# Router of a hybrid decoder layer: squares summed on VectorE, all expert groups ranked at once, bfloat16 counts, first rows picked on TensorE

## The chip, the cores and the metric

The program runs on one core of one Trainium2 chip, in one launch. The metric is the device time in microseconds (us) of that core. Engines are written as in the profile: PE is TensorE (PEld its weight loads), DVE is VectorE, ACT is ScalarE, POOL is GpSimd, SP is SyncE, which here issues most of the transfers. A trailing q (ACTq, SPq) marks the issue of a transfer.

## The reference, cut to what matters

One layer of a decoder on 264 tokens (256 of a prompt, 8 to be decoded) with 1024 channels. Two recurrent mixers run side by side, their outputs go through one projection of 2048 to 1024 and are added to the residual stream. Then comes the part that the change touches, a mixture of 16 experts in 4 groups of 4:

```python
def hier_moe(h, ...):                      # h = rmsnorm(x) * w_norm_ffn
    glog = (t @ w_rg).astype(f32)          # 264 x 4
    gprob = softmax(glog); gsel = argmax(glog + b_rg)
    gw = gprob at gsel
    elog = (t @ w_re) of the chosen group  # 264 x 4
    eprob = softmax(elog)
    _, topi = lax.top_k(elog + b_re[gsel], 2)
    ew = eprob at topi, divided by its sum
    gates = one_hot(4 * gsel + topi) * gw * ew
    act = silu(t @ w_gate[e]) * (t @ w_up[e]) * gates[e]     # 512 wide
    return sum over e of act @ w_down[e]
```

So each token chooses one group, then two of its four experts. After the experts a small gated embedding is added, and a last RMSNorm gives the output. All inputs and outputs are float32.

## The kernel before, in words

Each engine has its own program, written by hand; the order in the source is the order on the engine, and semaphores join them. Channels stand on the 128 partitions in most of the kernel: `xT`, `hT` and `sq` are 8 tiles (KT) of 128 x 264, one for each 128 channels. PSUM banks are handed out in turn: banks 0 to 3 go from PE to ACT (`a_full`, `a_took`), banks 4 to 7 from PE to DVE (`v_full`, `v_took`).

**Output projection (mix).** For each c of 8 output tiles PE multiplies 16 weight tiles into a bank (L1048, which appears as 32 instructions, two for each float32 product). DVE adds the bank to `xT[c]` and scales it into `hT[c]` (`weighted`); ACT writes the square of `xT[c]` to `sq[c]`. For the RMSNorm PE sums the squares over channels by a matrix of ones: `norm_part(1, c)`, L806, once for each of the 8 tiles, all into one bank. Four of these stand between the last mix tiles and four behind them, with the router's own products (`router_part`, L1067, 20 columns: 4 groups and 16 experts). ACT takes the root (L1364), PE turns the 1/rms factors and the router's logits so that tokens stand on partitions (L1102, L1074), and turns `hT` back to rows (`h_row`, L1094). ACT scales these rows into `htok`, two copies for each of three token tiles (L1572), and sends them to `h_rows` in HBM.

**Choice of experts.** DVE works on tiny arrays: 3 token tiles by 4 or 16 numbers on 128 partitions. `link` makes each instruction wait until the one before it has written. First the group is chosen (`first_max`: the maximum, who equals it, the first of these), then the four logits of that group are gathered, then the best and the second best are found, again with `first_max`. `Mt` holds for each token and expert whether it was chosen. PE counts with it (`cnt`, L1114): how many earlier tokens chose each expert, which is a token's slot there. Meanwhile DVE works out the gates and fills `rv`, the numbers that belong to each token and expert. Then, for each expert t, DVE compares slot numbers with 1 to 64 in two copies (`one_hots`, `OH`, 8 buffers) and PE multiplies `OH` with `rv` (`table`, L1123), which gives for every slot the token's row number and gate. Table 0 holds experts 0 and 1 (TAB0 = 2), table 1 the other 14. DVE copies each (L2023) and turns it into row numbers (`row_numbers`, semaphore `tab_ready`).

**Experts.** Up to 64 slots (CAP) for each expert. POOL gathers an expert's rows by an indirect transfer from `h_rows` into `xg` (L743) as half rows, 128 partitions of 512. PE turns them (`halves_rows`, L1235, bank 2 or 3), ACT copies them to `xgT` (L1540, `x_took`), PE multiplies with gate and up weights (`halves_gate_up`, L1226, `gu_full`), ACT and DVE make silu times up times gate, PE turns that and multiplies with the down weights (L1256, `d_full`). POOL scatters the result (L751). PE enters this phase by a wait for `v_took` of table 1.

**Weights.** An expert's three matrices are 6 MB. There are three slots (SLOTS). The first three experts' weights are asked for during the mix. From the fourth on SP waits for PE:

```python
for t in range(SLOTS, E):
    eng.wait_ge(main.gu_full, t - SLOTS + 1)
    load_gate(t)
    load_up(t)
    eng.wait_ge(main.d_full, t - SLOTS + 1)
    load_down(t)
```

## Time and profile before

| | us |
|---|---|
| median of 3 runs (lowest, highest) | 736.98 (734.15, 738.41) |
| time of the profiled execution | 739.89 |
| its span, first to last instruction | 738.1 |
| PE busy | 654.5 (89%) |
| PE weight loads busy | 451.9 (61%) |
| DVE busy | 297.4 (40%) |
| ACT busy | 178.8 (24%) |
| POOL busy | 82.3 (11%) |
| mean granted TensorE clock | 0.948 |

The time of an execution holds 1.8 us outside the span. Busy shares are means over stages with very different limits: the mixers and the projection lie before about 410 us, the router from there to 438.6 us, the experts from there to about 670 us, and the closing part behind them. A granted clock of 1.00 is TensorE's full 2.4 GHz, 0.50 is 1.2 GHz.

### The profile page before, as it was taken

The page shows a single profiled execution, that of the slowest core. Times are in us where ns is not written, and L with a number is a line of the kernel's source. Part 1 is how long each engine was busy: PE and PEld are TensorE (multiplying, and loading weights), DVE is VectorE, ACT ScalarE, POOL GpSimd, SP SyncE. Part 2 cuts the span into 40 slices and gives each one's busy share as a digit, 9 for nine tenths or more (in the row PEclk, how much of TensorE's full clock was granted, in tenths as well). Part 3 has the DMA queues.
Part 4 walks back from the last instruction along what each step waited for, and adds up shares of the span by engine and source line. Part 5 has one row for each costly group of instructions (what it writes and reads, how often), then busy time and mean ns, then how long its engine had stood idle before and what let it go on. Part 6 is the DMA issues. An engine that isn't in the chain of part 4 may idle for free. (4 is left out here: it accounts for less than half of the span.)

```text
span 738.1 us, 8341 instructions
## 1 busy us (share of the span) xinstructions
PE 654.5 (89%) x3225; PEld 451.9 (61%) x3225; DVE 297.4 (40%) x863; ACT 178.8 (24%) x417; POOL 82.3 (11%) x103
## 2 busy tenths in 40 slices
PE   4899999999998999999999759998877778786896
PEld 2688887787786988888877533332322223234685
DVE  0368277864449899845210570010001000010443
ACT  3222338312232232343300511010100000011323
POOL 5000024200012111100000010211111111001000
PEclk9999899999998999899999959999999999998899
DMA  9634258983023645535897705999999999996001
GB/s 252 232 114 133 97 176 282 345 266 132 1 88 103 214 131 180 166 92 172 342 377 306 284 25 235 407 422 423 424 423 422 421 427 422 426 398 222 0 1 59
DMA packets 44978, 177.92 MB, mean 241 GB/s; under 512 B 3989, under 2 KB 12633, under 8 KB 36608
## 3 DMA queue, kind: packets, MB, share of 16 engines
q1 hardware_dynamic: 34704, 147.21, 51.0%
q0 software_dynamic: 9712, 28.99, 12.7%
q10 hardware_dynamic: 520, 1.15, 0.4%
q8 instruction: 27, 0.44, 0.3%
q14 instruction: 15, 0.12, 0.0%
HBM read 165.48 MB, written 16.01 MB: 246 GB/s over the span
## 5 line engine op out<-in xcount | busy, mean ns | idle before, releaser
L830 PE MATMUL bank<-hT,arena 128*128 128x264 f32 x832 | 197.3, 398 | 5.7 <-DVE hT L1636 3.1
L830 PEld LDWEIGHTS bank<-hT,arena 128*128 128x128 f32 x832 | 161.9, 197 | 35.2 <-issue 5.6
L1226 PE MATMUL bank<-arena,hT 128*64 128x512 f32 x512 | 124.7, 643 | 31.0 <-DMA arena<-in_w_exp_up 30.4
L1226 PEld LDWEIGHTS bank<-arena,hT 128*64 128x64 f32 x512 | 42.2, 148 | 102.4 <-issue 100.7
L1628 DVE TENSOR_TENSOR arena<-arena 128x256 f32<-128x256 f32 (+8 forms) x149 | 60.2, 447 | 44.0 <-ACT arena L1441 20.4
L1636 DVE SCALAR_TENSOR_TENSOR hT<-hT,arena,bank 128x256 f32<-128x256 f32 x16 | 7.7, 481 | 158.8 <-ACT hT L1547 158.8
L1048 PE MATMUL bank<-arena 128*128 128x264 f32 x256 | 58.3, 387 | 1.3 <-issue 0.8
L1256 PE MATMUL bank<-arena,sq 128*64 128x512 f32 x256 | 58.4, 598 | 0.5 <-ACT sq L1552 0.5
L1048 PEld LDWEIGHTS bank<-arena 128*128 128x128 f32 x256 | 48.3, 190 | 10.6 <-issue 1.7
L1384 ACT ACTIVATE arena<-bank 128x264 f32<-128x264 f32 x44 | 17.1, 390 | 141.4 <-PE bank L830 141.3
L1547 ACT ACTIVATE hT<-bank 128x256 f32<-128x256 f32 x16 | 6.1, 384 | 147.8 <-PE bank L1226 147.8
L1636 DVE SCALAR_TENSOR_TENSOR arena<-arena 128x128 f32<-128x128 f32 (+1 forms) x130 | 35.5, 343 | 7.7 <-DMA arena<-in_state_ssm 7.5
L751 POOL DMA_INDIRECT pair_rows<-arena,rows x16 | 16.1, 1009 | 188.1 <-DVE arena L2093 188.1
L1256 PEld LDWEIGHTS bank<-arena,sq 128*64 128x64 f32 x256 | 17.3, 136 | 30.8 <-issue 30.1
L1628 DVE TENSOR_TENSOR arena<-bank,K 128x512 f32<-128x512 f32 (+1 forms) x34 | 22.4, 678 | 25.6 <-PE bank L975 15.3
L2093 DVE COPY arena<-bank 128x512 f32<-128x512 f32 x16 | 11.1, 692 | 52.3 <-PE bank L1256 52.3
L1314 PE MATMUL bank<-hT,arena 128*128 128x264 f32 x128 | 31.3, 405 | 0.0
L1855 DVE TENSOR_REDUCE arena<-arena 128x128 f32<-128x1024 f32 x16 | 30.5, 1904 | 0.0
L975 PE MATMUL bank<-arena 128*128 128x128 f32 x224 | 27.7, 275 | 1.5 <-DVE arena L1628 1.5
L1314 PEld LDWEIGHTS bank<-hT,arena 128*128 128x128 f32 x128 | 25.6, 201 | 4.7
L975 PEld LDWEIGHTS bank<-arena 128*128 128x128 f32 x224 | 26.8, 192 | 2.3 <-DVE arena L1628 1.9
L1636 DVE SCALAR_TENSOR_TENSOR arena<-arena,prm 128x253 f32<-128x253 f32 (+3 forms) x80 | 25.7, 365 | 2.4 <-ACT arena L1494 1.2
(252 smaller groups left out, 683.5 us busy)
## 6 DMA issues: line engine op xcount, KB each, us to landing
arena<-in_w_exp_gate SPq DMA_DIRECT2D x16, 2048.0 KB, 26.8
arena<-in_w_exp_up SPq DMA_DIRECT2D x16, 2048.0 KB, 31.2
arena<-in_w_exp_down SPq DMA_DIRECT2D x16, 2048.0 KB, 24.3
arena<-in_w_in SPq DMA_DIRECT2D x13, 2048.0 KB, 9.1
out<-arena POOLq DMA_DIRECT2D x18, 512.0 KB, 4.8
arena<-in_w_out SPq DMA_DIRECT2D x4, 2048.0 KB, 9.5
arena<-in_state_ssm POOLq DMA_DIRECT2D x8, 512.0 KB, 8.0
arena<-in_state_hgrn POOLq DMA_DIRECT2D x8, 512.0 KB, 4.5
```

The source lines that it names most:

```text
L751: eng.indirect_dma_start(out=pair_halves, out_offset=bass.IndirectOffsetOnAxis(ap=row_of[:, 1, t:t + 1], axis=0), in_=ys[:, p], in_offset= ...
L830: last = mm(ps[:, 0:T], w[:, k, j * P:(j + 1) * P], hT[:, k], start=(k == 0), stop=(k == KT - 1))
L975: last = mm(ps[:, j * P:(j + 1) * P], x, y, start=True, stop=True)
L1048: last = mm(ps[:, 0:T], w[:, k, (c % 2) * P:(c % 2) * P + P], x, start=(k == 0), stop=(k == 15))
L1226: last = mm(bank[p][r, :].rearrange("p (w f) -> p w f", w=2), xgT[:, p, k % 4, CAP * (k // 4):CAP * (k // 4) + CAP], gu[:, :, k, FF // 2 * ...
L1256: last = mm(bank[6 + p][r, :], actT[:, p, k % 2, CAP * (k // 2):CAP * (k // 2) + CAP], wd[:, k, HALF * c:HALF * (c + 1)], start=(k == 0), ...
L1314: last = mm(ps[:, 0:T], w[:, k, (c % 4) * P:(c % 4 + 1) * P], hT[:, k], start=(k == 0), stop=(k == KT - 1))
L1384: activation(PR[:, n], full("proj", n)[:, 0:T], func).then_inc(a_took, 1)
L1628: return nc.vector.tensor_tensor(out, a, b, op)
L1636: return nc.vector.scalar_tensor_tensor(out, a, s, b, op0, op1)
L1855: nc.vector.tensor_reduce(AT[:, h % 2, 256 * i:256 * i + P], LVt[:, i].rearrange("p a c -> p c a"), AX.X, ALU.add).then_inc(at_ready, 1)
L2093: nc.vector.tensor_copy(ys[:, p], bank[6 + p][:, :]).then_inc(main.d_took, 1)
```

## The change: what it does

1. `norm_part(1, c)` is gone. DVE adds `sq[1]` to `sq[7]` into `sq[0]` one by one (`add_square`, after ACT's square and with a semaphore `sq_sum` between them), and PE multiplies once with the ones.
2. `counting` is a bfloat16 copy of the two 128 x 128 matrices used for counting, made by DVE ahead of the mix. `Mt` is bfloat16 and has a fourth, empty tile. The count is four products with 64, 48, 32 and 16 columns in place of nine float32 products of 16.
3. DVE ranks the experts inside all four groups at once, on 48 numbers for each partition, while it ranks the groups; `pair` issues two independent instructions and waits for both. What belongs to the chosen group is masked out afterwards (`first`, `second`). The exponent's input of the expert softmax (`rs[:, 8]`, second `r_in`) comes behind the eleventh pair.
4. The slot numbers `slot1` are computed right behind the count, ahead of the gates.
5. The first expert's rows are neither gathered nor turned. DVE writes a one-hot matrix `first_hot` (3 token tiles x 64 slots, into `xg`), and PE multiplies the rows `htok` with it, 8 channel tiles x 3 token tiles = 24 float32 products of 64 columns, straight into bank 2. Half of them stand ahead of table 0, half behind it. They wait for ACT's last copy of `htok` and for `first_ready`. POOL no longer gathers for t = 0.

```diff
--- before.py
+++ after.py
@@ -344,11 +344,13 @@
         rv = carve(3 * E * RV // 2).bitcast(BF16).rearrange("p (t e c) -> p t e c", t=3, c=RV)
-        Mt = carve(3, E)
+        Mt = carve(4 * E // 2).bitcast(BF16).rearrange("p (t e) -> p t e", e=E)
...
         tabf = smalls[:, 0:3 * E * RV].rearrange("p (t c) -> p t c", c=RV)
+        counting = smalls[:, 3 * E * RV:3 * E * RV + P].bitcast(BF16)
+        first_hot = xg[:, 0, 0:3 * CAP].rearrange("p (t s) -> p t s", t=3)
@@ -356,6 +358,8 @@
         actT = sq_all[:, 1536:2048].rearrange("p (s k c) -> p s k c", s=2, k=2)
+        pick = [sq_all[:, 1536 + 3 * E * i:1536 + 3 * E * (i + 1)].rearrange("p (t g e) -> p t g e", t=3, g=EG)
+                for i in range(4)]
@@ -438,6 +442,7 @@
         sq_done, norm_done = sem("sq_done"), sem("norm_done")
+        sq_sum, counting_ready, first_ready = sem("sq_sum"), sem("counting_ready"), sem("first_ready")
@@ -758,7 +763,7 @@
                         eng.wait_ge(tab_ready, 2)
-                    if t < E:
+                    if 0 < t < E:
@@ -1077,14 +1082,14 @@
                 mix(c, range(16))
-                norm_part(1, c - 4)
...
                         router_part(k)
-            for c in range(4, KT):
-                if c >= 6:
-                    router_part(c)
-                norm_part(1, c)
+            for c in range(6, KT):
+                router_part(c)
+            ps = open_a("norm", 1)
+            eng.wait_ge(sq_sum, KT - 1)
+            mm(ps[:, 0:T], ones, sq[:, 0], start=True, stop=True).then_inc(a_full, 1)
@@ -1106,13 +1111,14 @@
-            eng.wait_ge(mt_ready, 3)
+            eng.wait_ge(counting_ready, 1)
+            eng.wait_ge(mt_ready, 2)
             ps = open_v("cnt")
-            for i in range(4):
-                c = slice(E * i, E * i + E)
-                for k in range(min(i + 1, 3)):
-                    last = mm(ps[:, c], ones if k < i else K[:, K_CAUSAL:K_CAUSAL + P], Mt[:, k],
-                              start=(k == 0), stop=(k == min(i, 2)))
+            up_to, every = counting[:, 0:P], counting[:, P:2 * P]
+            mm(ps[:, 0:4 * E], up_to, Mt[:, :, :], start=True, stop=False, skip_group_check=True)
+            for i in range(3):
+                last = mm(ps[:, E * (i + 1):4 * E].rearrange("p (t e) -> p t e", e=E), every,
+                          Mt[:, i:i + 1].to_broadcast([P, 3 - i, E]), start=False, stop=(i == 2), skip_group_check=True)
@@ -1123,7 +1129,16 @@
-            table(open_v("tab", 0), 0, TAB0, oh_ready, oh_used, v_full)
+            eng.wait_ge(a_took, ja["ht", 2, 1] + 1)
+            eng.wait_ge(first_ready, 1)
+            for k in range(KT):
+                if k == KT // 2:
+                    table(open_v("tab", 0), 0, TAB0, oh_ready, oh_used, v_full)
+                at = P * (k % 4) + CAP * (k // 4)
+                for i, (t0, n) in enumerate(TOK):
+                    last = mm(bank[2][:, at:at + CAP], htok[0:n, i, k * P:(k + 1) * P], first_hot[0:n, i],
+                              start=(i == 0), stop=(i == 2))
+            last.then_inc(main.x_full, 1)
@@ -1230,7 +1245,7 @@
                 p = t % 2
-                eng.wait_ge(main.rows[p], t // 2 * 16 + 16)
+                eng.wait_ge(main.rows[p], (t + p) // 2 * 16)
@@ -1259,7 +1274,6 @@
-                halves_rows(0)
@@ -1272,7 +1286,6 @@
-            eng.wait_ge(a_took, ja["ht", 2, 1] + 1)
@@ -1901,11 +1914,23 @@
                 tt(o[:, h], o[:, h], ms[:, h]).then_inc(mixed, 1)
+            eng.wait_ge(mixers_done, 1)
+            nc.vector.tensor_copy(counting, K[:, K_CAUSAL:K_CAUSAL + 2 * P]).then_inc(counting_ready, 1)
+            def add_square(c):
+                eng.wait_ge(sq_done, KT + c + 1)
+                if c > 1:
+                    eng.wait_ge(sq_sum, c - 1)
+                tt(sq[:, 0], sq[:, 0], sq[:, c], ALU.add).then_inc(sq_sum, 1)
...
                     weighted(c - 1, "mix", R_FFN)
+                if c >= 2:
+                    add_square(c - 1)
             weighted(KT - 1, "mix", R_FFN)
+            add_square(KT - 1)
@@ -1914,19 +1939,22 @@
-            def first_max(out, x, tmp, m):
-                red(m, x, ALU.max)
-                link(tt(tmp, x, bc(m), ALU.is_equal))
-                link(tt(tmp, tmp, w4))
-                red(m, tmp, ALU.max)
-                link(tt(out, tmp, bc(m), ALU.is_equal))
+            def pair(a, b, chain=dve):
+                for x in (a, b):
+                    own[chain] += 1
+                    x.then_inc(chain, 1)
+                eng.wait_ge(chain, own[chain])
+            def top(out, x, op):
+                return nc.vector.tensor_reduce(out, x, AX.X, op)
+            def of_group(x):
+                return x.rearrange("p t (g o) -> p t g o", o=1).to_broadcast([P, 3, EG, EPG])
...
             link(nc.vector.memset(rt[:, :, :], 0.0))
-            eng.wait_ge(mixers_done, 1)
-            for i in range(3):
-                link(nc.vector.memset(Mt[:, i], 0.0))
+            link(nc.vector.memset(Mt[:, :, :], 0.0))
@@ -1934,31 +1962,45 @@
             took("rt")
-            lg = rt[:, :, 0:4]
-            red(r1[:, 0], lg, ALU.max)
+            w16 = K[:, K_W4:K_W4 + 4].rearrange("p (o g e) -> p o g e", o=1, g=1).to_broadcast([P, 3, EG, EPG])
+            lg, ex = rt[:, :, 0:4], rt[:, :, 4:20].rearrange("p t (g e) -> p t g e", g=EG)
+            rbg = rb[:, 0:4].rearrange("p (o e) -> p o e", o=1).to_broadcast([P, 3, 4])
+            rbe = rb[:, 4:20].rearrange("p (o g e) -> p o g e", o=1, g=EG).to_broadcast([P, 3, EG, EPG])
+            biased, eq, first, second = pick
+            best, turn = rs[:, 11], rs[:, 12]
+            ohg = rs[:, 5]
+            ohb = ohg.rearrange("p t (g o) -> p t g o", o=1).to_broadcast([P, 3, EG, EPG])
+            g4 = gates[:, :, :].rearrange("p t (g e) -> p t g e", g=EG)
+            pair(top(r1[:, 0], lg, ALU.max), tt(biased, ex, rbe, ALU.add))
             tt(rs[:, 0], lg, bc(r1[:, 0]), ALU.subtract).then_inc(r_in, 1)
-            link(tt(rs[:, 3], lg, rb[:, 0:4].rearrange("p (o e) -> p o e", o=1).to_broadcast([P, 3, 4]), ALU.add))
-            ohg = rs[:, 5]
-            first_max(ohg, rs[:, 3], rs[:, 4], r1[:, 3])
-            g4 = gates[:, :, :].rearrange("p t (g e) -> p t g e", g=EG)
-            ohb = ohg.rearrange("p t (g o) -> p t g o", o=1).to_broadcast([P, 3, EG, EPG])
-            link(tt(g4, rt[:, :, 4:20].rearrange("p t (g e) -> p t g e", g=EG), ohb))
-            red(rs[:, 7], g4.rearrange("p t g e -> p t e g"), ALU.add)
-            link(tt(g4, rb[:, 4:20].rearrange("p (o g e) -> p o g e", o=1, g=EG).to_broadcast([P, 3, EG, EPG]), ohb))
-            red(rs[:, 14], g4.rearrange("p t g e -> p t e g"), ALU.add)
-            red(r1[:, 6], rs[:, 7], ALU.max)
+            pair(top(best, biased, ALU.max), tt(rs[:, 3], lg, rbg, ALU.add))
+            pair(tt(eq, biased, of_group(best), ALU.is_equal), top(r1[:, 3], rs[:, 3], ALU.max))
+            pair(tt(eq, eq, w16), tt(rs[:, 4], rs[:, 3], bc(r1[:, 3]), ALU.is_equal))
+            pair(top(turn, eq, ALU.max), tt(rs[:, 4], rs[:, 4], w4))
+            pair(tt(first, eq, of_group(turn), ALU.is_equal), top(r1[:, 4], rs[:, 4], ALU.max))
+            pair(stt(biased, first, -BIG, biased, ALU.mult, ALU.add), tt(ohg, rs[:, 4], bc(r1[:, 4]), ALU.is_equal))
+            pair(top(best, biased, ALU.max), tt(g4, ex, ohb))
+            pair(tt(eq, biased, of_group(best), ALU.is_equal), top(rs[:, 7], g4.rearrange("p t g e -> p t e g"), ALU.add))
+            pair(tt(eq, eq, w16), top(r1[:, 6], rs[:, 7], ALU.max))
+            pair(top(turn, eq, ALU.max), tt(first, first, ohb))
             tt(rs[:, 8], rs[:, 7], bc(r1[:, 6]), ALU.subtract).then_inc(r_in, 1)
-            link(tt(rs[:, 11], rs[:, 7], rs[:, 14], ALU.add))
-            first_max(rs[:, 12], rs[:, 11], rs[:, 4], r1[:, 3])
-            link(stt(rs[:, 13], rs[:, 12], -BIG, rs[:, 11], ALU.mult, ALU.add))
-            first_max(rs[:, 15], rs[:, 13], rs[:, 4], r1[:, 3])
-            link(tt(rs[:, 16], rs[:, 12], rs[:, 15], ALU.add))
-            chosen = rs[:, 16].rearrange("p t (o e) -> p t o e", o=1).to_broadcast([P, 3, EG, EPG])
-            for i, (t0, n) in enumerate(TOK):
-                tt(Mt[0:n, i].rearrange("p (g e) -> p g e", g=EG), ohb[0:n, i], chosen[0:n, i]).then_inc(mt_ready, 1)
+            link(tt(second, eq, of_group(turn), ALU.is_equal))
+            link(tt(second, second, ohb))
+            tt(Mt[:, 0:2].rearrange("p t (g e) -> p t g e", g=EG), first[:, 0:2], second[:, 0:2], ALU.add).then_inc(mt_ready, 1)
+            tt(Mt[0:NS, 2].rearrange("p (g e) -> p g e", g=EG), first[0:NS, 2], second[0:NS, 2], ALU.add).then_inc(mt_ready, 1)
+            ps = full("cnt")
+            eng.wait_ge(mt_ready, 2)
+            link(tt(slot1[:, :, :], ps[:, 0:3 * E].rearrange("p (t e) -> p t e", e=E), Mt[:, 0:3]))
+            eng.wait_ge(xg_clear, 2)
+            tt(first_hot, K[:, K_IOTA:K_IOTA + CAP].rearrange("p (o s) -> p o s", o=1).to_broadcast([P, 3, CAP]),
+               slot1[:, :, 0:1].to_broadcast([P, 3, CAP]), ALU.is_equal).then_inc(first_ready, 1)
+            nc.vector.tensor_reduce(most[:, :], ps[:, 3 * E:4 * E], AX.X, ALU.max).then_inc(v_took, 1)
+            took("cnt")
+            pair(top(rs[:, 15], second.rearrange("p t g e -> p t e g"), ALU.add),
+                 top(rs[:, 16], first.rearrange("p t g e -> p t e g"), ALU.add))
+            link(tt(rs[:, 16], rs[:, 16], rs[:, 15], ALU.add))
@@ -1991,12 +2033,6 @@
             link(tt(rv[:, :, :, 5], grest[:, :, :], rv[:, :, :, 4], ALU.subtract))
-            ps = full("cnt")
-            eng.wait_ge(mt_ready, 3)
-            tt(slot1[:, :, :], ps[:, 0:3 * E].rearrange("p (t e) -> p t e", e=E), Mt[:, :, :])
-            nc.vector.tensor_reduce(most[:, :], ps[:, 3 * E:4 * E], AX.X, ALU.max).then_inc(v_took, 1)
-            took("cnt")
...
```

On PE, at the end of the mix, before (L806 is a square tile times ones, L1067 a router product, L1048 the mix, L1094 the turning of `hT`):

```order
L1048 MATMUL bank<-arena 128x264 x16
L806 MATMUL bank<-sq,K 128x264
L1067 MATMUL bank<-hT,wr 20x264 x4
L1048 MATMUL bank<-arena 128x264 x16
L806 MATMUL bank<-sq,K 128x264
L1067 MATMUL bank<-hT,wr 20x264 x2
L806 MATMUL bank<-sq,K 128x264 x2
L1067 MATMUL bank<-hT,wr 20x264
L806 MATMUL bank<-sq,K 128x264
L1067 MATMUL bank<-hT,wr 20x264
L806 MATMUL bank<-sq,K 128x264
L1094 MATMUL bank<-K,hT 128x128 x8
```

and in the changed kernel, whose lines stand a little lower (L1053 is the mix, L1072 the router, L1092 the one product with ones):

```order
L1053 MATMUL bank<-arena 128x264 x96
L1072 MATMUL bank<-hT,wr 20x264 x4
L1053 MATMUL bank<-arena 128x264 x16
L1072 MATMUL bank<-hT,wr 20x264 x4
L1092 MATMUL bank<-sq,K 128x264
L1099 MATMUL bank<-K,hT 128x128 x8
```

Seven of eight products with ones are gone; the one that is left stands behind all router products.

On PE, between the turned rows and the first expert, before (L1114 count, L1123 tables, L1235 turning of the gathered rows, L1226 gate and up of expert 0):

```order
L1094 MATMUL bank<-K,hT 8x128 x8
L1114 MATMUL bank<-arena,K 128x16 x9
L1123 MATMUL bank<-arena,sq 128x8 x48
L1235 MATMUL bank<-K,arena 128x128 x4
L1226 MATMUL bank<-arena,hT 64x512 x16
```

and in the changed kernel (L1118 and L1120 count, L1139 picks, L1129 tables, L1241 gate and up of expert 0):

```order
L1099 MATMUL bank<-K,hT 8x128 x8
L1118 MATMUL bank<-arena 128x64
L1120 MATMUL bank<-arena 128x48
L1120 MATMUL bank<-arena 128x32
L1120 MATMUL bank<-arena 128x16
L1139 MATMUL bank<-arena 128x64 x12
L1129 MATMUL bank<-arena,sq 128x8 x6
L1139 MATMUL bank<-arena 128x64 x12
L1129 MATMUL bank<-arena,sq 128x8 x42
L1241 MATMUL bank<-arena,hT 64x512 x16
```

The turning of the gathered rows has gone from in front of gate and up, and 24 picks have come in around table 0, whose result DVE waits for.

On DVE, at the start of the choice, before (L1915 is a reduction, `rs` and `r` hold 4 or 1 numbers for each token tile):

```order
L1915 TENSOR_REDUCE r<-rt 128x3
L1628 TENSOR_TENSOR rs<-rt,r 128x12
L1628 TENSOR_TENSOR rs<-rt,rb 128x12
L1915 TENSOR_REDUCE r<-rs 128x3
L1628 TENSOR_TENSOR rs<-rs,r 128x12
L1628 TENSOR_TENSOR rs<-rs,K 128x12
L1915 TENSOR_REDUCE r<-rs 128x3
L1628 TENSOR_TENSOR rs<-rs,r 128x12
L1628 TENSOR_TENSOR gates<-rt,rs 128x48
```

and in the changed kernel (`sq` holds the 48 numbers of all groups):

```order
L1950 TENSOR_REDUCE r<-rt 128x3
L1641 TENSOR_TENSOR sq<-rt,rb 128x48
L1641 TENSOR_TENSOR rs<-rt,r 128x12
L1950 TENSOR_REDUCE rs<-sq 128x12
L1641 TENSOR_TENSOR rs<-rt,rb 128x12
L1641 TENSOR_TENSOR sq<-sq,rs 128x48
L1950 TENSOR_REDUCE r<-rs 128x3
L1641 TENSOR_TENSOR sq<-sq,K 128x48
L1641 TENSOR_TENSOR rs<-rs,r 128x12
L1950 TENSOR_REDUCE rs<-sq 128x12
```

Between two steps of the group's choice now stands a step of the experts' choice.

## Rows read from the trace of the kernel before

**Rows 1.** Waits, 455 to 738 us: engine, line, waited for, us, times, longest

```profile
PE bank L1226 <- DMA arena<-in_w_exp_up: 30.4, 10, 4.2
```

**Rows 2.** Stretches of 5 us: engines' busy us, PEclk, DMA share, GB/s

```profile
465.00:470.00 5.00, 5.00 (x26) 1.76 (x24) 0.48 (x1) 0.98 (x2) 0.00 (x0) 1.00 1.04 437
```

**Rows 3.** Timeline, end of the mix: start us, us, engine line op

```profile
392.32 6.05 PE L1048 MATMUL bank<-arena 128*128 128x264 f32 x26 [0.42 <-DMA arena<-in_w_out]
...
399.55 0.61 PE L806 MATMUL bank<-sq,K 128*128 128x264 f32 x2
...
400.08 1.96 PE L1067 MATMUL bank<-hT,wr 128*20 128x264 f32 x8
...
401.97 6.97 PEld L1048 LDWEIGHTS bank<-arena 128*128 128x128 f32 x32 [0.43 <-issue]
401.97 7.39 PE L1048 MATMUL bank<-arena 128*128 128x264 f32 x32
...
409.39 0.43 DVE L1628 TENSOR_TENSOR xT<-xT,bank 128x264 f32<-128x264 f32 x1 [8.95 <-PE bank L1048]
...
413.56 0.71 PE L806 MATMUL bank<-sq,K 128*128 128x264 f32 x2
```

**Rows 4.** Timeline, DVE in the router

```profile
416.20 0.17 DVE L1915 TENSOR_REDUCE r<-rt 128x3 f32<-128x12 f32 x1
...
417.70 0.21 DVE L1628 TENSOR_TENSOR gates<-rt,rs 128x48 f32<-128x48 f32 x1
...
421.66 0.33 DVE L1628 TENSOR_TENSOR arena<-rs 128x16 f32<-128x16 f32 x3
...
426.83 0.21 DVE L1628 TENSOR_TENSOR arena<-bank,arena 128x48 f32<-128x48 f32 x1
426.95 0.17 DVE L1997 TENSOR_REDUCE most<-bank 128x1 int32<-128x16 f32 x1
427.15 1.50 DVE L1628 TENSOR_TENSOR sq<-K,arena 128x384 bf16<-128x384 f32 x3
```

**Rows 5.** Timeline, ACT in the router

```profile
416.73 2.00 ACT L1572 ACTIVATE arena<-bank,rtok 128x512 f32<-128x512 f32 x2
...
419.17 0.21 ACT L1568 ACTIVATE rs<-rs 128x12 f32<-128x12 f32 x1 [0.45 <-DVE rs L1628]
...
421.72 2.01 ACT L1572 ACTIVATE arena<-bank,rtok 8x512 f32<-8x512 f32 x2 [0.43 <-ACT arena L1572]
```

**Rows 6.** Timeline, float32 products with 16 columns, and two small weight loads

```profile
71.04 4.98 PE L854 MATMUL bank<-arena,hT 128*128 128x16 f32 x48
...
415.08 0.20 PEld L1102 LDWEIGHTS bank<-K,rstd 20*128 20x128 f32 x3 [0.17 <-issue]
...
415.23 0.20 PEld L1074 LDWEIGHTS bank<-K,rstd 1*128 1x128 f32 x3
...
422.05 4.02 PE L1114 MATMUL bank<-arena,K 128*128 128x16 f32 x18 [2.67 <-DVE arena L1628]
```

**Rows 7.** Stretches of 2 us

```profile
420.00:422.00 2.00, 0.00 (x0) 0.00 (x0) 1.70 (x12) 1.57 (x3) 0.00 (x0) 0.96 0.99 412
422.00:424.00 2.00, 1.95 (x10) 1.96 (x10) 1.66 (x11) 1.73 (x2) 0.00 (x0) 0.50 0.84 344
...
442.00:444.00 2.00, 2.00 (x12) 0.72 (x10) 0.00 (x0) 0.00 (x0) 0.00 (x0) 0.92 0.00 0
```

**Rows 8.** Timeline, tables and first expert

```profile
428.56 0.17 DVE L2023 COPY arena<-bank 128x16 f32<-128x16 f32 x1
...
429.99 6.18 DVE L1628 TENSOR_TENSOR sq<-K,arena 128x384 bf16<-128x384 f32 x13
...
436.50 0.28 DVE L2023 COPY arena<-bank 128x112 f32<-128x112 f32 x1 [0.34 <-PE bank L1123]
...
438.65 8.88 PE L1226 MATMUL bank<-arena,hT 128*64 128x512 f32 x32 [0.69 <-ACT hT L1540]
...
447.57 0.33 SPq L535 DMA_DIRECT2D arena<-in_w_exp_gate  x1
```

## The prediction, written before the changed kernel was run

> **What bounds the kernel now.** I read the waits of the last 280 us first. TensorE waits for expert weights ten times, 30.4 us in all [rows 1], and from 465 us on the DMA engines are full at 437 GB/s [rows 2]: the expert phase is bound by the transfer of weights. These transfers have a start, though. SP asks for the fourth expert's weights only when gate and up of expert 0 are done: the product starts at 438.65, takes 8.88, and SP issues at 447.57 [rows 8]. Until then the queues are empty: 0 GB/s from 442 to 444 [rows 7]. So whatever moves the end of that product moves the whole expert phase, and the closing part behind it, by as much. The router in front of it is one chain: the last mix tile (DVE takes it at 409.39), root and turned factors, DVE's choice from 416.20 to 421.99, its gates until 426.83, the one-hots from 427.15, table 1's copy at 436.50, turning of the first rows, expert 0 at 438.65 [rows 3, 4, 8]. DVE has hardly a gap in it. The question is how much of this chain goes, and what the new work on TensorE puts in its place.
>
> **Squares on VectorE.** A product with ones costs 0.53 in the stream, 399.55 to 400.08 [rows 3]. Three of them lie before the last mix tile ends. Two are in front of tile 6, which waits for its weights anyway (0.42 idle before 392.32), so they give nothing; the third gives 0.53, and DVE takes the last tile at 408.86. Behind it stand, on DVE, add to xT, scale, add square, scale, add square. Such instructions follow each other by 0.35 and last 0.43 (the row at 409.39), so the last sum is there at 408.86 + 4 x 0.35 + 0.43 = 410.7. TensorE's router products end at about 410.85, held by the last scale. The one product with ones takes 0.71 as the last one did [rows 3]: done at 411.5 in place of 414.27. Root, turned rows and factors follow in the same order as before, so DVE starts choosing at 416.20 - 2.77 = 413.43. The seven adds and the bfloat16 copy of the masks lie in DVE's idle time (8.95 us before the last tile alone) except for the last two adds, which are counted.
>
> **Choosing in all groups.** Before, 5.46 from 416.20 to 421.66, then 0.33 for Mt [rows 4]. Now eleven pairs and four single steps. A second independent instruction starts 0.12 after the first (426.83 and 426.95), one on 48 numbers lasts 0.21, one on 12 lasts 0.17, and the wait between links adds 0.035; a pair is 0.33 to 0.39, eleven of them 3.8. With the two inputs for ACT (0.09 each), two single steps (0.49) and Mt (0.3) that makes 4.8: Mt stands at 418.2, 3.8 earlier than before's 421.99, of which 1.0 is from here. The reductions over 48 numbers for 12 results may cost 0.1 more each, six of them: bounds 0.4 and 1.2 gained.
>
> **Counting.** Eighteen instructions with 4.02 us [rows 6] become four. Before, DVE did not wait for them: it came to `slot1` at 426.83, when they had ended (426.07). Now DVE waits for the count at once: about 0.6 from Mt to the first read (nearest: a one-hot to its table's copy takes 0.9 for six products). Then slot1, the one-hot of 192 columns (0.3), the maximum, one pair and one step: DVE is at 420.15. The gates and `rv` follow as before, 421.99 to 426.83, 4.84: one-hots start at about 425.0 in place of 427.15. **2.1 gained so far**, less than the 3.8 of Mt, since the wait for the count and the new steps now stand in the chain.
>
> **Picking the first rows.** The four products that turned them, the copy on ACT and its hand-over go from behind table 1: 436.88 to 438.65, about 1.75 less about 0.15 for the hand-over of table 1 that remains, 1.6 gained. The picks are the price. They wait for ACT's last copy of `htok`. ACT waits for the second `r_in` before it goes on with tile 1; that comes behind the eleventh pair, at 417.5. From there to the end of the last copy took 4.56 before (419.17 to 423.73, [rows 5]), so the picks start at 422.15. TensorE has been almost idle for five microseconds by then. Before, the granted clock fell from 1.00 to 0.50, 2.4 to 1.2 GHz, just before 422 after less idleness, and came back only at 442.3, inside expert 0 [rows 7]. So I put the picks at the low clock. A float32 product is two instructions; with 128 x 128 weights and few columns each took 0.22 at the low clock (18 in 4.02) and 0.104 at the high one (48 in 4.98) [rows 6]. Twelve products, 24 instructions: 5.2 us. Table 0 can start at 427.4, though DVE has its two one-hots ready at 426.0: DVE gets the table at 428.0 instead of 426.5 and loses **1.5**. The rest: 428.0 + 1.43 for row numbers (428.56 to 429.99, [rows 8]) = 429.4, then 13 one-hots. The second half of the picks ends at 433.2, and DVE's eighth of these waits for a free buffer until table 1 has started, 0.75 more. Last one-hot 436.4, last table product 436.65, copy, expert 0 at 437.05 in place of 438.65.
>
> The third token tile has only 8 rows. The two small loads [rows 6] take 0.20 with 20 rows and with 1 row alike, so I count its picks in full. The Trainium skill (TensorE: Matmul & The Clock Gate, "LDWEIGHTS") has the same rule, that a load's time goes by its columns and not by its rows. If rows counted, a half would be 16 instructions, 3.5 us, DVE would not wait and the gain would be 3.4.
>
> **Sum.** 2.1 (mix, root, choice, count) + 1.6 (turning) - 1.5 (table 0 late) - 0.75 (buffers) + 0.15 (rounding, table 0's own slack) = **1.6 us** off the start of expert 0. Its own clock I take as before. 739.89 - 1.6 = 738.3 for the profiled execution, which stands 2.9 above the median of 736.98; on the median that is **735.4**. POOL's missing gather gives nothing: the second one has the 8.88 of expert 0's product to land in. The earlier request for weights changes nothing but its time.
>
> **Rivals.**
> - *The picks bring the clock back.* They are ten microseconds of unbroken work, and 64 columns are four times those of the count. For it: the clock came back at 442.3 in the middle of unbroken products of 512 columns [rows 7]. Against it: the count's 4.02 unbroken microseconds left it at 0.50 [rows 6, 7]. If it rises near the first half's end, the second takes 2.5, no buffer is missed, DVE loses 1.0 or less, and expert 0 starts 2.5 to 3.8 earlier, itself up to 1.8 shorter (half of the 3.65 from 438.65 to 442.3, which it ran at the low clock): 4.5 gained, 732.5. The Trainium skill ("What's actually happening" of the same page) says that the low clock is the default and activity releases it, which speaks for this rival.
> - *Weight loads do not hide behind the picks (slower).* In the mix 6.97 of loads lie beside 7.39 of products [rows 3], so there they do. At 64 columns and the low clock an instruction would be 0.20 + 0.11 = 0.30. Then a half takes 7.3 us, table 0 ends at 430.0, the second half at 437.3, DVE waits with its eighth one-hot until 437.6, and expert 0 starts at 441.1, 2.4 later: 739.4. It decides from 0.25 on per instruction.
> - *The transfer hides it.* If the weights' total time and not their start set the end, nothing would move: 737.0. Against it are the empty queues before 447.57 [rows 7, 8].
>
> **How the numbers follow.** Forecast 0.62, clock back 0.14, loads unhidden 0.10, hidden 0.07, the rest for the unforeseen on both sides. Within the forecast the unknown costs (reductions, count, pick at 0.20 to 0.24) make 0 to 3.5 gained: 733.5 to 737. The two first rivals and the spread of the three runs shown, 4.3 us, widen it to 731.3 to 739.2. Half a per cent, 3.7 us, is about what a measurement of this kernel tells from no change. Faster by more: most of the clock rival (0.10) and the forecast's lower end (0.15). Slower by more: the upper end of the second rival, 0.05. Same: 0.70.
>
> **What would show it.** In the changed profile: L1092 once, ending some 2.8 before the old place relative to the last mix tile; Mt to first table read; L1139 at 0.50 clock, 24 + 24 instructions of 0.22, starting right behind the last L1572 copy's counterpart on ACT; DVE's first table copy waiting for PE for 1.5; the eighth one-hot of the second lot waiting; expert 0's gate and up 1.6 earlier relative to the last mix tile; SP's fourth gate weights right behind it; and PE's waits for weights of the same sum. I am wrong if the picks run at 0.104, if DVE does not wait for table 0, or if expert 0 moves and the end does not.

## The result, and the profile after

The changed kernel takes 738.99 us (median of 20 runs, 735.94 to 742.75), the kernel before 736.75 in the same comparison: ratio 1.0038, 95% interval 1.002 to 1.0055, so **2.8 us slower** (1.5 to 4.1; the two medians by themselves differ by 2.2). Ratios here and below leave out runs more than 1.5% above the fastest of the same kernel: five of the thirteen of "all warmed, 128 rows", at most one of any other. The time lies in the range given, and the loss is within the half per cent that I called no change; but I had worked out a gain of 1.6 us, and the sign was wrong.

Timeline of the changed kernel, router to first expert (columns as in [rows 3]), against [rows 3, 4, 5, 8]:

```profile
389.56 7.39 PE L1053 MATMUL bank<-arena 128*128 128x264 f32 x32 [1.31 <-DMA arena<-in_w_out]
...
406.19 0.43 DVE L1641 TENSOR_TENSOR xT<-xT,bank 128x264 f32<-128x264 f32 x1 [8.16 <-PE bank L1053]
...
408.11 0.71 PE L1092 MATMUL bank<-sq,K 128*128 128x264 f32 x2
...
410.74 0.17 DVE L1950 TENSOR_REDUCE r<-rt 128x3 f32<-128x12 f32 x1
...
415.03 0.26 DVE L1641 TENSOR_TENSOR arena<-sq 128x32 bf16<-128x32 f32 x2
...
417.22 1.99 ACT L1585 ACTIVATE arena<-bank,rtok 8x512 f32<-8x512 f32 x2 [0.42 <-ACT arena L1585]
...
419.26 6.71 PE L1139 MATMUL bank<-arena 128*128 128x64 f32 x24 [3.58 <-ACT arena L1585]
...
421.97 1.50 DVE L1641 TENSOR_TENSOR sq<-K,arena 128x384 bf16<-128x384 f32 x3
...
426.08 6.69 PE L1139 MATMUL bank<-arena 128*128 128x64 f32 x24
426.26 0.17 DVE L2059 COPY arena<-bank 128x16 f32<-128x16 f32 x1 [2.79 <-PE bank L1129]
427.69 3.36 DVE L1641 TENSOR_TENSOR sq<-K,arena 128x384 bf16<-128x384 f32 x7
...
432.98 2.90 DVE L1641 TENSOR_TENSOR sq<-K,arena 128x384 bf16<-128x384 f32 x6 [1.93 <-PE bank L1129]
...
436.21 0.28 DVE L2059 COPY arena<-bank 128x112 f32<-128x112 f32 x1 [0.33 <-PE bank L1129]
...
436.54 9.89 PE L1241 MATMUL bank<-arena,hT 128*64 128x512 f32 x32 [0.37 <-DVE arena L2059]
...
446.47 0.33 SPq L540 DMA_DIRECT2D arena<-in_w_exp_gate  x1
```

Absolute times mislead here. The last mix tile (second row) comes at 406.19, in before's profile at 409.39, though nothing changed ahead of it but squares worth half a microsecond. It came anywhere from 405.3 to 412.7 in the profiled runs of this study, at 405.36, 406.19, 406.55 and 407.70 in four of one and the same kernel. So I measure from that row. The squares' own share is read from mix tile 6's start (first row, 389.56) to this row: 17.07 us before, 16.63 after, **0.44 earlier**.

| stretch, us | before | after |
|---|---|---|
| start to the last mix tile at DVE | 409.39 | 406.19 |
| to the start of expert 0's gate and up | 29.26 | 30.35 |
| gate and up of expert 0 | 8.88 | 9.89 |
| to the first add of pairs at the end | 234.62 | 237.79 |
| closing part | 55.95 | 54.18 |
| span | 738.1 | 738.4 |

The last two stretches tell nothing of the change. The one before the closing part is taken up below. The closing part took 53.00 to 56.05 in four profiles of the kernel before with no edit and 53.08 to 54.59 in four of the changed one.

The second stretch is the change's own: 1.09 later, less the 0.44, makes **0.65 later** instead of 1.6 earlier. The picks start where forecast (13.07 behind the mix tile, forecast 13.29), but the first 24 instructions take 6.71 us, not 5.2, and DVE waits 2.79 for table 0 and 1.93 for a buffer, not 1.5 and 0.75.

Stretches of the same profile (2 us, then 5), against [rows 7] and [rows 2]: the clock is 0.50 from before the picks (it fell at 414.9, 4.3 us ahead of them) into expert 0, where it came back at 442.2, and behind it the transfer is full again. PE waits for weights as in [rows 1].

```profile
422.00:424.00 2.00, 2.00 (x9) 1.76 (x8) 1.47 (x3) 0.00 (x0) 0.00 (x0) 0.50 0.02 8
...
440.00:442.00 2.00, 2.00 (x8) 0.71 (x6) 0.00 (x0) 0.00 (x0) 0.00 (x0) 0.50 0.21 55
442.00:444.00 2.00, 2.00 (x10) 0.56 (x8) 0.00 (x0) 0.00 (x0) 0.00 (x0) 0.94 0.00 0
...
465.00:470.00 5.00, 5.00 (x26) 1.76 (x24) 0.48 (x1) 0.98 (x2) 0.00 (x0) 1.00 1.06 447
```

```profile
PE bank L1241 <- DMA arena<-in_w_exp_up: 30.4, 10, 4.2
```

TensorE's groups by shape from 419 to 433 us (busy us, mean ns of one; neighbours overlap, so that a mean is longer than a step). The weight tile of a pick is a piece of `htok`, one row for each token: 32 instructions have 128 rows, 16 have 8, those of the third token tile. PEld is the loading of these tiles.

```profile
L1139 PE MATMUL bank<-arena 128*128 128x64 f32 x32 | 8.9, 434 | 3.6 <-ACT arena L1585 3.6
L1139 PE MATMUL bank<-arena 8*128 8x64 f32 x16 | 5.5, 444 | 0.0
```

```profile
L1139 PEld LDWEIGHTS bank<-arena 128*128 128x128 f32 x32 | 7.4, 322 | 4.4 <-ACT arena L1585 3.7
L1139 PEld LDWEIGHTS bank<-arena 8*128 8x128 f32 x16 | 4.0, 308 | 0.9
```

The starts of single instructions say more. Four of 128 rows: 419.26, 419.53, 419.74, 419.96; two of 8 rows: 420.31, 420.58; the next of 128 rows: 420.92, 421.19, 421.40, 421.62; then 8 rows at 421.97. As long as the height (the number of rows) stays 128, neighbours are 0.21 apart. Where the height changes the step is 0.35, and the one behind it 0.27: 0.2 us lost at each change. Seven changes lie in 24 instructions. The loads show where it is lost: one of 8 rows lasts as long as one of 128 (308 and 322 ns), but within equal heights a load starts 0.21 behind the one before it and 0.10 ahead of its own product, while at a change it starts 0.45 behind the one before it and only together with its own product (420.31). The loss is in the overlap of the load with the product before it, not in the load's own time.

### The profile page after: what moved, and what is told of

Same layout as the page of the kernel before. It is cut to its first block and busy times, and to the rows that moved or that the text cites. A ratio compares the mean times of both kernels' runs of the same rounds, so it can differ in the third digit from the quotient of the medians.

```text
span 738.4 us, 8387 instructions
## 1 busy us (share of the span) xinstructions
PE 656.7 (89%) x3241; PEld 453.8 (61%) x3241; DVE 299.5 (41%) x871; ACT 178.7 (24%) x417; POOL 81.3 (11%) x102
## 5 line engine op out<-in xcount | busy, mean ns | idle before, releaser
L835 PE MATMUL bank<-hT,arena 128*128 128x264 f32 x832 | 193.9, 393 | 5.6 <-DVE hT L1649 3.1
L835 PEld LDWEIGHTS bank<-hT,arena 128*128 128x128 f32 x832 | 159.6, 194 | 34.0 <-issue 3.5
L1241 PE MATMUL bank<-arena,hT 128*64 128x512 f32 x512 | 128.8, 661 | 30.8 <-DMA arena<-in_w_exp_up 30.4
L1241 PEld LDWEIGHTS bank<-arena,hT 128*64 128x64 f32 x512 | 43.5, 151 | 104.5 <-issue 103.5
L1053 PE MATMUL bank<-arena 128*128 128x264 f32 x256 | 58.1, 387 | 2.3 <-DMA arena<-in_w_out 1.3
L1053 PEld LDWEIGHTS bank<-arena 128*128 128x128 f32 x256 | 48.3, 190 | 11.6 <-issue 1.8
L2129 DVE COPY arena<-bank 128x512 f32<-128x512 f32 x16 | 11.1, 691 | 52.3 <-PE bank L1271 52.3
L1327 PE MATMUL bank<-hT,arena 128*128 128x264 f32 x128 | 29.4, 387 | 0.0
L1327 PEld LDWEIGHTS bank<-hT,arena 128*128 128x128 f32 x128 | 24.2, 190 | 4.1
```

The lines of the kernel that those rows point to most:

```text
L835: last = mm(ps[:, 0:T], w[:, k, j * P:(j + 1) * P], hT[:, k], start=(k == 0), stop=(k == KT - 1))
L1053: last = mm(ps[:, 0:T], w[:, k, (c % 2) * P:(c % 2) * P + P], x, start=(k == 0), stop=(k == 15))
L1241: last = mm(bank[p][r, :].rearrange("p (w f) -> p w f", w=2), xgT[:, p, k % 4, CAP * (k // 4):CAP * (k // 4) + CAP], gu[:, :, k, FF // 2 * ...
L1327: last = mm(ps[:, 0:T], w[:, k, (c % 4) * P:(c % 4 + 1) * P], hT[:, k], start=(k == 0), stop=(k == KT - 1))
L2129: nc.vector.tensor_copy(ys[:, p], bank[6 + p][:, :]).then_inc(main.d_took, 1)
```

## The experiments

All in the table ran against the kernel before in three timings, 12 or 13 runs of each against 35 of the kernel before (medians 737.76, 738.00 and 737.79; medians are of all runs). The ratio, and not a difference of medians, is what compares them. "Start" is expert 0's start behind the last mix tile; "net" is that start against before's 29.26, less the 0.44 of the squares where they are on VectorE.

| kernel | median us | ratio, 95% interval | start | net |
|---|---|---|---|---|
| picks with 128 rows | 734.91 | 0.9975 (0.9945 to 1.0004) | 27.48 | -2.2 |
| no picks | 733.55 | 0.9946 (0.9913 to 0.9979) | 27.07 | -2.6 |
| squares back on TensorE | 740.75 | 1.0025 (0.9999 to 1.0050) | 32.60 | +3.3 |
| no picks, DVE delayed | 738.41 | 0.9982 (0.9951 to 1.0013) | 30.38 | +0.7 |
| picks warmed | 737.10 | 0.9970 (0.9942 to 0.9999) | 28.78 | -0.9 |
| no picks, warmed | 739.24 | 0.9995 (0.9966 to 1.0024) | 29.68 | 0.0 |
| all warmed, 128 rows | 738.33 | 1.0012 (0.9983 to 1.0041) | 25.43 | -4.3 |
| changed, unedited | 738.84 | 1.0017 (0.9989 to 1.0046) | 30.36 | +0.7 |
| before, unedited | 736.41 | 0.9986 (0.9952 to 1.0021) | 29.25 | 0.0 |
| **picks 128 rows, spread** | 733.43 | **0.9926 (0.9897 to 0.9954)** | 26.09 | -3.6 |

**Picks with 128 rows.** The third token tile's picks read all 128 rows; the added ones meet zeros in the one-hot.

```
-  mm(bank[2][:, at:at + CAP], htok[0:n, i, k * P:(k + 1) * P], first_hot[0:n, i],
+  mm(bank[2][:, at:at + CAP], htok[0:P, i, k * P:(k + 1) * P], first_hot[0:P, i],
```

> The changed kernel with one edit: the third token tile of each pick is taken with all 128 rows instead of 8 (the 120 rows more are multiplied by zeros of the one-hot matrix). Theory A: an instruction of the picks costs 0.213 us as long as the row count stays the same, and each change between a 128-row and an 8-row weight tile, sixteen of them, costs 0.2 us more. Then 24 instructions take 5.2 us in place of 6.7, the wait of VectorE for table 0 falls from 2.8 to about 1.3 us, and expert 0 starts 2 to 2.5 us earlier behind the last mix tile (30.35 us in the changed kernel): 28.1. Theory B: products of 64 columns cost 0.28 each at the low clock whatever the rows: 6.7 us as before, nothing moves. Time: A about 2 us under the changed kernel, B the same as it (0.4% over the kernel before).

```profile
419.12 5.38 PE L1139 MATMUL bank<-arena 128*128 128x64 f32 x24 [3.58 <-ACT arena L1585]
...
424.68 0.17 DVE L2059 COPY arena<-bank 128x16 f32<-128x16 f32 x1 [1.34 <-PE bank L1129]
...
429.96 2.90 DVE L1641 TENSOR_TENSOR sq<-K,arena 128x384 bf16<-128x384 f32 x6 [0.43 <-PE bank L1129]
...
433.53 9.54 PE L1241 MATMUL bank<-arena,hT 128*64 128x512 f32 x32 [0.37 <-DVE arena L2059]
```

More rows, less time: 24 instructions in 5.38 (0.22 each, the forecast's price), 1.33 less than 6.71, which is 0.19 for each of seven changes of height. The clock was 0.50 in both. The loads' idle time in front of them is gone but for the start:

```profile
L1139 PEld LDWEIGHTS bank<-arena 128*128 128x128 f32 x48 | 10.4, 331 | 3.7 <-ACT arena L1585 3.7
```

DVE's waits fall by 1.45 and 1.50, and expert 0 starts 2.87 earlier: the changes of height are the whole miss at the start of expert 0 (2.2), and the waits stand where I had put them (1.34 and 0.43 against 1.5 and 0.75). The time followed: ratio 0.9975, where the changed kernel had 1.0038 in the first timing and 1.0017 in the table. No run has more than two instructions of 8 rows side by side, so what a longer run of them costs isn't known.

**No picks.** Picks, their one-hot and their order are out; gather and turning of expert 0's rows are back. Squares, choice and count stay as changed.

```
-                    if 0 < t < E:
+                    if t < E:
...
+                halves_rows(0)
```

> The changed kernel with the picks taken out again: expert 0's rows are gathered and turned as before, all the rest of the change stays. If the picks are what costs, table 0 is not delayed, VectorE makes its one-hots without a break and expert 0 starts 27.3 us behind the last mix tile (30.35 in the changed kernel, 29.26 before): 1.9 us less than the kernel before plus 0.4 from the mix, so 2.3 us or 0.3% faster than before. If the loss sits elsewhere (the squares on VectorE, the choice), it stays slower than before by 1 to 3 us.

Timeline of this kernel: the one-hots run on without a wait, and the turning (1.09 and its hand-over) is back in front of expert 0.

```profile
425.60 1.50 DVE L1634 TENSOR_TENSOR sq<-K,arena 128x384 bf16<-128x384 f32 x3
...
428.44 6.23 DVE L1634 TENSOR_TENSOR sq<-K,arena 128x384 bf16<-128x384 f32 x13
...
435.38 1.09 PE L1241 MATMUL bank<-K,arena 128*128 128x128 f32 x4 [0.41 <-issue]
```

Start 27.07, 3.3 earlier than with the picks. The rest of the change alone makes the kernel 0.54% faster (0.2 to 0.9); the picks take it back.

**Squares back on TensorE**, all else as changed:

```
+                norm_part(1, c - 4)
...
-            ps = open_a("norm", 1)
-            eng.wait_ge(sq_sum, KT - 1)
-            mm(ps[:, 0:T], ones, sq[:, 0], start=True, stop=True).then_inc(a_full, 1)
```

> The changed kernel with the squares summed on TensorE again (eight products with ones instead of seven additions on VectorE and one product). By the prediction's step the sum comes 2.2 us later behind the last mix tile and the tile 0.4 later: expert 0 starts at 32.5 behind the last mix tile instead of 30.35, time 2.7 us or 0.36% above the changed kernel. Rival: the picks wait for ScalarE and not for this chain, so that part of it is hidden: under 1 us.

Start 32.60, 2.25 later than the changed kernel, and the mix tile 0.44 later. The last product with ones ends 4.88 behind the mix tile, as in [rows 3] (414.27 - 409.39); with the sums on VectorE it is 2.63:

```profile
412.61 0.43 DVE L1641 TENSOR_TENSOR xT<-xT,bank 128x264 f32<-128x264 f32 x1 [8.95 <-PE bank L1053]
...
416.78 0.71 PE L811 MATMUL bank<-sq,K 128*128 128x264 f32 x2
```

**Does the time follow the start?** Without picks, DVE is held back by sixteen linked copies that nothing uses, so that expert 0 starts when it does in the changed kernel:

```
+            for _ in range(16):
+                link(nc.vector.tensor_copy(rs[:, 0], rs[:, 16]))
             one_hots(0, TAB0 + 1, oh_ready, oh_used, iota_halves)
```

> The changed kernel without picks, with sixteen linked copies of 12 numbers on VectorE ahead of the one-hots (0.2 us each, their result is not used), which put expert 0's start back from 27.07 to 30.35 behind the last mix tile, where the changed kernel has it. Start theory: the time follows the start alone, so this one is as slow as the changed kernel, 3.3 us above the one without picks (0.9946), at 0.998 to 1.001 of the kernel before. Rival (the picks cost something more, later): it stays 2 us or more below the changed kernel.

```profile
422.69 3.30 DVE L2069 COPY rs<-rs 128x12 f32<-128x12 f32 x16
```

The start came at 30.38 as meant, and the ratio rose from 0.9946 to 0.9982 in another timing, the way of the start, but by less than the errors of the two together (0.0045). Clearer is the same timing's best version, further down: its start is 4.3 us earlier than this one's and its ratio 0.0056 lower, 4.1 us, beyond the errors (0.0042). So the start counts. Whether the picks have a second cost isn't told: with the same start the changed kernel stood 0.0035 (2.6 us) higher beside this one, which is the rival's number, but no more than the errors of the two. The unedited pair of that timing:

> The changed kernel once more, unedited, as the measure for the three beside it on the same chip. By the start of expert 0 (1.1 us later behind the last mix tile, which comes 0.4 earlier) it should be 0.65 us or 0.1% slower than the kernel before; by its first timing 0.38%. Start theory: 0.1%, and the first timing was at the end of its spread. Rival: something else in it costs 2 us more, then 0.3 to 0.5% again.

> The kernel before against itself. It shows how far two equal kernels can stand apart in such a timing: ratio 1.000, and if it lies beyond 0.2% from 1, the 0.38% of the changed kernel are not all its own. Its profile gives one more sample of the clock of the last expert.

Those two stand 1.0017 and 0.9986 against one baseline: the same 0.3% apart as in the first timing, each within its error of nothing. Four more profiled runs, two of each kernel (736.32 and 738.20 changed, 738.58 and 734.78 before), gave starts of 30.36, 30.36, 29.28 and 29.28. Over five profiles of each kernel **the start repeats within 0.06 us while the time wanders by 4**. What was expected of the first of them:

> The changed kernel unedited, a profile only. In three profiles of it so far expert 0's gate and up took 9.4 to 9.9 us, in three with the kernel before's start 8.5 to 8.9; if that belongs to the kernel, it is over 9.2 again. The last expert at the low clock or not decides 3 us of the span; if it belongs to the changed kernel, it is low more often than before.

**The clock.** Products of 248 columns whose results nobody reads fill TensorE's idle time ahead of the picks:

```
+            def keep_busy(n):
+                for _ in range(n):
+                    mm(bank[4][:, 264:512], K[:, K_LM:K_LM + P], K[:, K_LM + P:K_LM + P + 248], start=True, stop=True)
...
+            keep_busy(7)
```

> The changed kernel with thirteen idle products of 248 columns (0.41 us each at the high clock) in TensorE's gaps between the first turned rows and the picks; their results are not used. Theory A: the picks are slow because the clock has fallen after TensorE stood idle, and because of the change of rows. At the high clock a pick instruction is 0.107 and the change about 0.1 more: 24 in 3.4 instead of 6.7 us, table 0 is not delayed, no buffer is waited for, expert 0 starts at 25.5 us behind the last mix tile instead of 30.35. Theory B: the clock is not what costs, the picks take 6.7 as before and expert 0 starts at 30.3. Time: A 4 to 5 us below the changed kernel, 0.3% below the one before; B as the changed kernel or slower.

```profile
420.00:422.00 2.00, 1.52 (x10) 1.34 (x10) 1.79 (x13) 0.43 (x1) 0.00 (x0) 1.00 1.01 414
422.00:424.00 2.00, 2.00 (x10) 1.68 (x9) 1.86 (x6) 0.00 (x0) 0.00 (x0) 0.65 0.26 102
424.00:426.00 2.00, 2.00 (x14) 1.76 (x14) 0.75 (x3) 0.00 (x0) 0.00 (x0) 0.50 0.04 8
```

The picks began at the high clock (1.00, that is 2.4 GHz), and it fell to 0.50 in the middle of them, with PE busy through that stretch. The first 24 instructions took 5.10 and the second 6.69; start 28.78, 1.6 earlier. While the clock was high, the steps were 0.11 within 128 rows, 0.20 at a change of height and 0.16 behind it, so a change cost 0.14 us there. The next one adds 128 rows, a product ahead of each of table 1's turns, and six ahead of the weights of each of experts 6 to 15:

> The same with the third token tile taken with 128 rows, with one idle product of 128 columns ahead of each of table 1's last 13 turns and six ahead of experts 6 to 15 (all unused). If clock and row change are the two prices of the picks: 24 instructions in 2.6 us, expert 0 starts at about 25.4 us behind the last mix tile and takes 7.1 instead of 9.9, its end 32.5 behind the last mix tile in place of 40.2 (38.1 before); the last expert at the high clock. Time: 5 to 7 us or 0.7 to 0.9% below the kernel before. If the idle products get in the way of the tables, expert 0 starts at 27 or later and half of that is lost.

```profile
419.73 2.89 PE L1150 MATMUL bank<-arena 128*128 128x64 f32 x24 [0.63 <-ACT arena L1598]
...
432.03 7.09 PE L1254 MATMUL bank<-arena,hT 128*64 128x512 f32 x32 [0.37 <-DVE arena L2072]
```

Its profiled run held 1.00 through the router, the picks included, and through the experts until 661.8, and took 727.8 us; its twelve others took 736.8 to 745.5. So 25.43 is the start of one run with the clock held, and not what this kernel gets. Why the twelve were slower no profile shows; the next kernel's profile shows what can happen. Without picks the same filling lost its clock at 431.4, and the idle product ahead of each of table 1's turns took 0.77. The turns then came 0.69 apart, 0.47 without idle products, and DVE waited 3.04 for table 1's copy (0.34 without). That took back what the missing picks had won:

> The changed kernel without picks (expert 0's rows gathered and turned) and with the idle products in the gaps, in table 1 and ahead of experts 6 to 15. It tells what the picks are worth when the clock is held: rows turned at the high clock cost 1.4 us behind table 1, so expert 0 starts at 26.7 behind the last mix tile, 1.3 later than with picks, and takes 7.1. If the picks are worth their place once the clock is high, this one is 1.3 us slower than the one with picks; if they are never worth it, it is the same or faster.

**The end of the experts.** In the changed kernel's profile the last expert ran at the low clock, in before's at the high one:

```profile
651.53 9.91 PE L1241 MATMUL bank<-arena,hT 128*64 128x512 f32 x32 [3.39 <-DMA arena<-in_w_exp_up]
...
684.22 3.48 DVE L1641 TENSOR_TENSOR arena<-arena 128x1024 f32<-128x1024 f32 x3 [14.04 <-DMA arena<-pair_rows]
```

The same two rows of before:

```profile
652.37 7.09 PE L1226 MATMUL bank<-arena,hT 128*64 128x512 f32 x32 [1.92 <-DMA arena<-in_w_exp_up]
...
682.15 3.48 DVE L1628 TENSOR_TENSOR arena<-arena 128x1024 f32<-128x1024 f32 x3 [13.96 <-DMA arena<-pair_rows]
```

From expert 0's end to the adds is 236.7 to 237.8 us wherever the last expert took 8.8 to 9.9, and 233.7 to 235.5 wherever it took 7.1. Is that the change's doing? Six idle products ahead of the weights of experts 6 to 15, in either kernel:

```
+                for _ in range(6 if t >= 6 else 0):
+                    mm(bank[p][:, 0:248], K[:, K_LM:K_LM + P], K[:, K_LM + P:K_LM + P + 248], start=True, stop=True)
                 eng.wait_ge(main.wg[s], turn * 16 + 16)
```

> The changed kernel with six idle products of 248 columns in front of gate and up of experts 6 to 15, written to a bank that is overwritten next; their results are not used. In the changed kernel's profile the last expert ran at the low clock (9.9 us of gate and up in place of 7.1), in that of the kernel before at the high clock. Theory T: a good part of the 2.8 us lost is this clock of the last expert. The products fill the wait for weights, the clock stays high, and the last expert takes 7.1 in both kernels: this one then is 1 to 3 us faster than the changed kernel and at about the same time as the kernel before, or faster. Rival: the clock in the expert phase averages out over runs, all of the loss lies ahead of expert 0; then this one still stands 1 to 3 us behind the same edit of the kernel before, and the two with the edit differ as the two without it (0.38%).

> The kernel before with the same idle products in front of gate and up of experts 6 to 15. The last expert was at the high clock in the profile of before already, but in other runs it need not be. Theory T: the gain over the kernel before is small (under 1.5 us), and the changed kernel with this edit is 0.5 to 1.7 us slower than this one (the later start of expert 0) instead of 2.8. Rival: the two differ by 2.8 us as without the edit. If the products only cost their time, the kernel gets slower by up to 2.5 us.

They gave 736.36 (1.0011, 0.9977 to 1.0045) and 738.16 (0.9999, 0.9964 to 1.0035), both with the last expert at 7.1: nothing that shows beyond the errors. And with no edit, the last expert took 8.8 in two of before's three other profiles and 7.1 in all three others of the changed kernel. So nothing ties it to the change; it varies between runs of one kernel, and the two groups of profiles stand 2.7 us apart on the mean.

**The best version: picks spread.** With 128 rows, and in pieces: three of the eight column blocks ahead of table 0, the others between table 1's turns, where TensorE waits for one-hots.

```
+            picks(0, 3)
+            table(open_v("tab", 0), 0, TAB0, oh_ready, oh_used, v_full)
+            picks(3, 5)
+            ps = open_v("tab", 1)
+            table(ps, TAB0, 5, oh_ready, oh_used, oh_used)
+            picks(5, 6)
+            table(ps, 5, 8, oh_ready, oh_used, oh_used)
+            picks(6, 8).then_inc(main.x_full, 1)
+            table(ps, 8, E, oh_ready, oh_used, v_full)
```

> The changed kernel with all picks at 128 rows and spread: three channel tiles ahead of table 0 (3.84 us at 0.213 each, done when VectorE's second one-hot is), then two, turns 2 to 4 of table 1, one, turns 5 to 7, two, turns 8 to 15. VectorE then waits neither for table 0 nor for a buffer, and the rows need no turning: expert 0 starts 25.9 us behind the last mix tile, against 27.07 without picks, 27.48 with picks at 128 rows in two halves, 29.26 before. Time 3.8 us or 0.5% below the kernel before, 1.2 us below the one without picks. If the picks' row count and their place are not what costs, it stays at 27.5 or above.

```profile
405.44 0.43 DVE L1651 TENSOR_TENSOR xT<-xT,bank 128x264 f32<-128x264 f32 x1 [8.16 <-PE bank L1053]
...
418.97 4.11 PE L1140 MATMUL bank<-arena 128*128 128x64 f32 x18 [3.58 <-ACT arena L1595]
...
423.26 0.17 DVE L2069 COPY arena<-bank 128x16 f32<-128x16 f32 x1
...
424.69 6.17 DVE L1651 TENSOR_TENSOR sq<-K,arena 128x384 bf16<-128x384 f32 x13
...
431.20 0.27 DVE L2069 COPY arena<-bank 128x112 f32<-128x112 f32 x1 [0.34 <-PE bank L1130]
431.53 8.54 PE L1251 MATMUL bank<-arena,hT 128*64 128x512 f32 x32 [0.37 <-DVE arena L2069]
```

DVE finds table 0 ready (no wait in brackets) and makes its 13 one-hots in one piece, as in [rows 8]. Start 26.09, 4.27 earlier than changed: 733.43 us, ratio 0.9926, faster than both kernels. From the kernel without picks (0.9946 in another timing) the time doesn't tell it apart; its start is 0.98 earlier.

## Why the prediction was wrong, point by point

- **Squares, right.** Norm done 2.63 behind the mix tile (forecast 2.64); the tile 0.44 earlier (0.53). Putting the squares back costs 2.25 behind the tile; forecast 2.77 less 0.53, 2.24.
- **Choice and count, right.** DVE starts choosing 4.55 behind the tile (forecast 4.57), Mt stands at 9.1 (9.3), the one-hots start at 15.78 (16.1; before 17.76).
- **Turning gone, right.** Table 1's copy to expert 0 is 0.33 in place of 2.15: 1.8 gained, 1.6 forecast.
- **The clock at the picks, right**, and the rival that they bring it back wrong: 0.50 through 48 instructions, 13.5 us without a gap, and on into expert 0. The fall came earlier than before: 8.7 us behind the mix tile (8.3 to 11.1 in five profiles) and not 12.4 (11.1 to 12.4).
- **The price of the picks, the failed step.** I wrote: "The third token tile has only 8 rows ... so I count its picks in full." That rested on two rows of 0.20 [rows 6], read as one load each; each row is three loads side by side, and a single one of 128 columns took 0.13 there with 20 rows and with 1. The inference stands all the same: in the picks a load took 322 ns with 128 rows and 308 with 8. The Trainium skill (TensorE: Matmul & The Clock Gate, "LDWEIGHTS") says that a load's time goes by its columns and not by its rows, and this trace agrees. What the step left out is the neighbour, that is, the overlap: where tiles of 128 and of 8 rows take turns, the load behind a change does not run ahead, and each change costs 0.2 us more. That is 1.4 us in 24 instructions, 0.28 on the mean in place of 0.22. The term "5.2 us" was 6.71; with it table 0 (1.5 forecast, 2.79) and the buffer (0.75, 1.93) came 2.5 us later together. DVE came 0.36 earlier than forecast to the one-hots, so expert 0 started 2.2 later than forecast (30.35 against 437.05 - 408.86 = 28.19).
- **Expert 0's own length, a term put at nothing.** I wrote: "Its own clock I take as before." It took 9.89 in place of 8.88 in the first pair of profiles, and 9.71 against 8.94 on the mean of five each: 0.8 more. In all seventeen profiles in which the clock came back inside expert 0, its length is 7.05 us and half of the time from its start to that return, to 0.01. The return came 4.6 to 5.7 us behind its start in the five of the changed kernel, and 2.9 to 3.7 in four of before's five, 5.7 in the fifth.
- **A sum beside the forecast.** With 16 instructions to a half the gain by my own terms is 2.1 + 1.6 = 3.7, not 3.4; nothing hangs on it.
- **The slower rival** is half right. It said that it decides from 0.25 per instruction on, and 0.28 is beyond that; but the loads fail to hide only at the changes of height, and hide between equal ones (0.22). Its price of 7.3 us for a half was too high (6.71). Its 2.4 us of time are near the 2.8 measured by luck: it had expert 0 start 2.4 later, and that was 0.65.
- **The end follows the start, borne out in size and not to the tenth.** Nets of -3.6, -2.6, -2.2 and +3.3 us gave -5.5, -4.0, -1.8 and +1.8 us (ratios by 737 us), each with some 2 us of error; with the best version clearly faster, the rival that the transfer hides the start is out. Three don't fit well: the delayed kernel (+0.7 gave -1.3) within its error, the changed one (+0.7 gave +2.8 in the first timing, +1.3 in the second), and the warmed one with 128 rows (-4.3 gave +0.9), whose profiled run was unlike the others. "Picks warmed" (-0.9 gave -2.2) is within its error.

**What stays open.** The start explains 0.65 of the 2.8 us. Expert 0 itself took 9.35 to 9.89 in five profiles of the changed kernel, mean 9.71, and 8.48 to 9.90, mean 8.94, in five of before (one of each five with the idle products, which come later): 0.8 more, which makes 1.4 at its end, just under the interval of the first timing (1.5 to 4.1) and inside the second's (1.0017: -0.8 to 3.4). Whether the later return of the clock in expert 0 belongs to the change isn't settled: before had 9.90 once, the kernel without picks 9.96, the spread one 8.54. The remaining 1.4 us has no place in these profiles: between expert 0's end and the adds the four profiles of each kernel with no edit take 235.6 us (changed) and 236.0 (before) on the mean.

## What to carry to other kernels

Keep the height of the weight tiles the same along a run of small products, and pad a short tile with rows that meet zeros rather than cut it: 128 rows were cheaper than 8 in between. When work is put ahead of a product that another engine waits for, cut it into pieces and lay them where that engine has work of its own; the picks cost 3.3 us in two lumps of uneven height, 0.4 in two of even height, and less than nothing when spread (27.07 without them, 26.09 with). And compare the stretch that the change touches from a common mark: it repeated within 0.06 us, while 0.3% of the whole time took twenty runs to see.
